# Grouped-query scores of the first block as three split products, their halves made in the second gate stage

## The reference, cut to what matters

```
def attend(q, k, v, scale):
    s = jnp.einsum("bqkgd,blkd->bkgql", q, k).astype(jnp.float32) * scale
    p = jax.nn.softmax(s, axis=-1).astype(v.dtype)
    return jnp.einsum("bkgql,blkd->bqkgd", p, v)
...
    k_gqa = rms_norm(k_g.reshape(b, l, GQA_KV_HEADS, GQA_DIM), lp["g_kn_gqa"])
    q_gqa = rms_norm(q_g.reshape(b, l, GQA_HEADS, GQA_DIM), lp["g_qn_gqa"])
...
    oc_gqa = attend(qc_gqa, k_gqa_c, v_gqa_c, GQA_DIM ** -0.5)
```

## Time and profile before

| | |
|---|---|
| time, median of 3 runs (lowest, highest) | 2534.72 us (2531.97, 2537.26) |
| profiled execution: span from first to last instruction | 2534.4 us |
| profiled execution: own time | not listed apart from its span |
| TensorE busy | 2434.9 us, 96% |
| VectorE busy | 1635.4 us, 65% |
| ScalarE busy | 1318.0 us, 52% |
| GpSimd busy | 405.1 us, 16% |
| mean granted TensorE clock | 0.993 of full |

### The profile page before, as it was taken

One profiled execution on the slowest core, in us unless ns is written; L12 is line 12 of the kernel. 1 busy time (PEld: TensorE's weight loads), 2 busy tenths in 40 slices (PEclk: granted clock), 3 DMA queues, 4 the chain that ended last, 5 costly groups with the idle time before them and its releaser, 6 DMA issues. The chain is left out here.

```text
span 2534.4 us, 45823 instructions
## 1 busy us (share of the span) xinstructions
PE 2434.9 (96%) x17406; PEld 2158.2 (85%) x17406; DVE 1635.4 (65%) x2537; ACT 1318.0 (52%) x2157; POOL 405.1 (16%) x354
## 2 busy tenths in 40 slices
PE   6999999999899999999999999998999999999997
PEld 5876899898599988875899899887998799769986
DVE  3664787567577857774788466546665666576655
ACT  3444566454546645545466455445554554465544
POOL 1210211221031121111301211020110211011102
PEclk9999999999999999999999999999999999999999
DMA  8576466566245655474556566563466466535663
GB/s 277 187 228 213 152 192 193 167 190 205 78 134 175 200 168 162 151 241 164 161 182 192 175 219 201 163 207 109 136 198 199 150 199 203 162 101 161 195 202 116
DMA packets 332956, 450.43 MB, mean 178 GB/s; under 512 B 28192, under 2 KB 207392, under 8 KB 332768
## 3 DMA queue, kind: packets, MB, share of 16 engines
q1 hardware_dynamic: 332400, 446.32, 55.9%
q0 software_dynamic: 368, 1.57, 0.2%
HBM read 446.73 MB, written 1.05 MB: 177 GB/s over the span
## 5 line engine op out<-in xcount | busy, mean ns | idle before, releaser
L771 DVE TENSOR_TENSOR wlo<-raw,whi 128x1024 fp32r<-128x1024 f32 (+2 forms) x706 | 845.2, 1215 | 589.4 <-ACT whi L765 585.4
L765 ACT CAST whi<-raw 128x1024 fp32r<-128x1024 f32 (+2 forms) x776 | 768.1, 1007 | 637.2 <-PE S L1065 233.7
L1086 PE MATMUL S<-hhi,whi 128*128 128x256 f32 x1943 | 538.4, 277 | 1.4 <-ACT b_kT L1394 0.9
L1086 PE MATMUL S<-hlo,whi 128*128 128x256 f32 x1943 | 536.5, 277 | 1.2 <-DVE hlo L2054 1.1
L1086 PE MATMUL S<-hhi,wlo 128*128 128x256 f32 x1943 | 536.5, 277 | 0.0
L1086 PEld LDWEIGHTS S<-hhi,whi 128*128 128x128 f32 x1943 | 365.2, 188 | 2.4 <-ACT b_kT L1394 1.1
L1086 PEld LDWEIGHTS S<-hlo,whi 128*128 128x128 f32 x1943 | 365.1, 188 | 1.8 <-DVE hlo L2054 1.7
L1086 PEld LDWEIGHTS S<-hhi,wlo 128*128 128x128 f32 x1943 | 365.1, 188 | 0.0
L1086 PE MATMUL G<-hhi,whi 128*128 128x256 f32 x1084 | 301.1, 278 | 0.4 <-ACT hhi L1456 0.4
L1086 PE MATMUL G<-hlo,whi 128*128 128x256 f32 x1084 | 298.1, 278 | 0.1
L1086 PE MATMUL G<-hhi,wlo 128*128 128x256 f32 x1084 | 297.9, 277 | 0.0
(11 more groups left out here) (404 smaller groups left out, 4336.0 us busy)
## 6 DMA issues: line engine op xcount, KB each, us to landing
raw<-in_ffn_wi SPq DMA_DIRECT2D x352, 256.0 KB, 3.5
raw<-in_w_up SPq DMA_DIRECT2D x264, 256.0 KB, 3.8
modw<-in_w_mod SPq DMA_DIRECT2D x192, 256.0 KB, 4.6
raw<-in_w_in SPq DMA_DIRECT2D x192, 256.0 KB, 3.0
raw<-in_ffn_wo SPq DMA_DIRECT2D x160, 256.0 KB, 3.5
raw<-in_w_down SPq DMA_DIRECT2D x120, 256.0 KB, 3.5
raw<-in_a_wqkv SPq DMA_DIRECT2D x72, 256.0 KB, 3.1
raw<-in_w_o SPq DMA_DIRECT2D x48, 256.0 KB, 3.2
```

The source lines that it names most:

```text
L765: act.copy(whi[:, n0 % SPLIT, z, w], raw[:, n0 % RAW, z, w]).then_inc(hi_done, 1)
L771: eng.tensor_tensor(wlo[:, n0 % SPLIT, z, w], raw[:, n0 % RAW, z, w], whi[:, n0 % SPLIT, z, w].bitcast(F32), ALU.subtract)\
L1086: mm = pe.matmul(o, w, x, start=first and c == 0 and m == 0 and z == 0, stop=last and c == kc - 1 and z == len(terms) - 1, skip_group_chec ...
```

## The change

The grouped keys and queries get high and low halves of their own. On ScalarE, at the start of the second gate stage and ahead of its first slot, two casts make `kghi` and `qghi`; they wait until the products of `uq` and the transposes of `gqat` are done. On VectorE, in the same stage behind the nine low halves of the weights and ahead of the rest of the row work, two subtractions make the low halves, in place of `kgT` and `qgT` (for the context, whose keys are needed again by the latent stream, the keys' low half goes to the second half of `kghi`). Both high halves lie in memory that is free between `uq` and the Fourier product behind the attention. In the attention the score of a grouped head is the sum of three fp32r products, (high q, high k), (high q, low k), (low q, high k), alternating between the two heads; one wait for `grouped_lo` is added ahead of them, the wait for `exp_done` is the same as before. The latent heads are unchanged.

```diff
@@ tensors
+            ("kghi", 0, [P, 4 * T], F32R), ("qghi", 7 * T, [P, GQA_H // 2, T], F32R),
...
+             ("b1_qglo", o1["qgT"], [P, GQA_H // 2, T], F32R),
+             ("b1_kglo", o1["kgT"], [P, GQA_KV, 2 * T], F32R),
@@ helper
+        def grouped_keys(st):
+
+
+            x = kgT[:, :, 0:st.blocks * P]
+            if st.s == LAT:
+                return x, kghi[:, :].rearrange("p (e n) -> p e n", e=GQA_KV), kglo[:, :, :]
+            both = kghi[:, :].rearrange("p (z e n) -> p z e n", z=2, e=GQA_KV)
+            return x, both[:, 0], both[:, 1]
@@ TensorE, attention
+                def grouped_scores(s):
+
+
+                    c, g = pairs_[s // 2][1], 2 * pairs_[s // 2][1] // (GQA_H // GQA_KV)
+                    rows_q = slice(s % 2 * P, (s % 2 + 1) * P)
+                    _, k_hi, k_lo = grouped_keys(st)
+                    pe.wait_ge(grouped_lo, 2 * owns.index(st) + 2)
+                    pe.wait_ge(exp_done, 2 * (st.a + s - 1))
+                    for z, (q, k) in enumerate(((qghi, k_hi), (qghi, k_lo), (qglo, k_hi))):
+                        for j in range(2):
+                            lo, s0 = slice(j * DH, (j + 1) * DH), (2 * (s % 2) + j) * SN
+                            mm = pe.matmul(S[:, s0:s0 + nb * P], q[lo, c, rows_q], k[lo, g], start=z == 0, stop=z == 2,
+                                           skip_group_check=True)
+                    mm.then_inc(s_done, 1)
...
                     name, c, _ = pairs_[s // 2]
+                    if name == "gqa":
+                        grouped_scores(s)
+                        return
...
-                        elif name == "gqa":
-                            parts.append([(qgT[lo, c, rows_q], kgT[lo, 2 * c // (GQA_H // GQA_KV), 0:nb * P])])
@@ ScalarE, gates
+                    if st.part:
+
+                        uq, gqat = before(st, "uq"), before(st, "gqat")
+                        act.wait_ge(bank_done[1], uq.n + uq.counts["n"])
+                        for q in range(gqat.tk, gqat.tk + gqat.counts["tk"]):
+                            act.wait_ge(tr_free[q % 2], q // 2 + 1)
+                        keys, k_hi, _ = grouped_keys(own_of(st))
+                        act.copy(k_hi, keys).then_inc(grouped_hi, 1)
+                        act.copy(qghi[:, :, :], qgT[:, :, :]).then_inc(grouped_hi, 1)
@@ VectorE, gates
                     over_units(dve, st, lambda k, j, i: split_weights(st, j, i, k, lo_and_rows))
+                    if st.part:
+                        own = own_of(st)
+                        keys, k_hi, k_lo = grouped_keys(own)
+                        for z, (x, hi, to) in enumerate(((keys, k_hi, k_lo), (qgT[:, :, :], qghi[:, :, :], qglo[:, :, :]))):
+                            dve.wait_ge(grouped_hi, 2 * owns.index(own) + z + 1)
+                            dve.tensor_tensor(to, x, hi.bitcast(F32), ALU.subtract).then_inc(grouped_lo, 1)
                     for _ in rows_work:
                         pass
```

More of the change, by code:

```diff
@@ L425, in build @@
             ("modw", 0, [P, 2 * MOD_SLOTS, SK, SN], F32)])
-        xn, gtB, crT, av, rsB, diag2, junk = region(3 * D, [
+        xn, gtB, crT, av, rsB, diag2, kghi, qghi, junk = region(3 * D, [
             ("xn", 0, [P, NT, D], F32), ("gtB", NT * D, [P, D], F32), ("crT", 0, [P, 2, 5, T], F32R),
             ("av", 0, [P, 2, 2, T], F32), ("rsB", 4 * T, [P, T], F32), ("diag2", 5 * T, [P, NT, P], F32),
+            ("kghi", 0, [P, 4 * T], F32R), ("qghi", 7 * T, [P, GQA_H // 2, T], F32R),
             ("junk", 6 * T, [P, 2, T], F32)])
@@ L448, in build @@
         o2, n2 = offsets(sizes)
-        (qkv1, qT1, qgT, gT, kT1, kgT, v1, vg, oThi1, oTlo1, fThi1, fTlo1,
+        (qkv1, qT1, qgT, gT, kT1, kgT, v1, vg, qglo, kglo, oThi1, oTlo1, fThi1, fTlo1,
          qkvA, qkvB, kdupB, sgate, sgained, qT2, kT2, sm, mask, order, pT, phi, plo, oThi2, oTlo2, fThi2, fTlo2) = region(max(n1, n2), [
@@ L547, in build @@
         exp_done = sem("exp_done")
+        grouped_hi = sem("grouped_hi")
+        grouped_lo = sem("grouped_lo")
         rden_ready = sem("rden_ready")
@@ L639, in follows_mod, with own_of @@
             return st.kind == "gates" and st.part == 1
+        def own_of(st):
+            return next(z for z in STAGES[STAGES.index(st):] if z.kind == "attn")
+        owns = [st for st in STAGES if st.kind == "attn" and st.name == "own"]
+        def grouped_keys(st):
[4 more added lines that the diff above has]
+            return x, both[:, 0], both[:, 1]
         def value_bank(st, p):
```

## The result

The changed kernel takes 2547.88 us (median of 5 runs, 2546.47 to 2548.76); the kernel before, measured beside it, 2534.72 us (2531.97 to 2542.36). The ratio is 1.0051, with a 95% interval of 1.004 to 1.0061: 13 us slower, between 10 and 15.5. The recorded execution spans 2546.1 us against 2534.4, 11.7 more. The device time of an execution is a little longer than its span: 2547.88 against 2546.1 here, and by 1.8 to 2.1 us in the executions of the kernel before whose span is known. So the recorded execution of the kernel before took about 2536.3 us (an estimate from that difference), 1.6 us more than the median; its span can't be set against the median as was done ahead. This would explain why the spans differ by less than the medians.

The account below looks back on a forecast made before the run. TensorE, busy for 96% of the span, was taken as the bound. Waits of +10.1, scores of -2.0 and clock of +3.0 us sum to +11.1 on the recorded 2534.4: 2545.5 us, range 2538.5 to 2551.5.

Parts of the forecast that it names:

- Casts on the chain: Second gate stage: ScalarE's two new casts start VectorE's chain 1.9 us later in each latent stream, 1.5 in the context.
- Subtractions on the chain: VectorE, ahead of the last row work: two subtractions add 2.4 us in each latent stream, hidden in the context.
- The latent seam: Between second gate stage and attention: `rows_ready` comes 4.3 us later, all paid by TensorE, twice, 8.6 us.
- Scores: Grouped attention steps on TensorE: three split products save 0.15 us (latent) or 0.06 (context) a step, 2.0 us in all.
- Clock: TensorE's clock falls to half in or behind the wait at both latent seams, 1.5 us each, +3.0 us.
- the first: Rival: no new fall of the clock at the latent seams; +8.1 us, 2542.5 us, chance 0.15.
- the fifth: Rival: casts and subtractions fall into gaps at the seam and only the saving is left; 2532.4 us, chance 0.03.
- The second: Rival: grouped scores on TensorE pay back 8.2 us, clock kept; +1.9 us, 2536.3 us, not slower, chance 0.14.
- The third: Rival: grouped products run one behind another, steps grow by 0.32 and 0.08 us; +16.8 us, 2551.2 us, chance 0.08.
- the fourth: Rival: weight loads of grouped products are not hidden, 0.42 and 0.51 us lost; +21.2 us, 2555.6 us, chance 0.04.

Follow-up runs that it names:

- the two kernels with halves in gaps: The change with casts late on ScalarE, subtractions on VectorE behind its parts of attention steps 0 and 2: 2534.87 us with split products, 2534.48 with two fp32 products.
- the run with GpSimd: The change with casts late on ScalarE and subtractions moved from VectorE to GpSimd: 2544.14 us, ratio 1.0036 to the kernel before.

## Why the prediction was right

The time predicted was 2545.5 us, slower; measured were 2547.88, inside the range. The 2545.5 were counted from the recorded span, so the number to set beside it is the span of the changed kernel, 2546.1. Step by step, by the two recorded executions:

- **Casts on the chain.** 1.9 us predicted for the first low half in the latent stream, 1.90 measured (3.16 - 1.26). In the context 1.5 predicted; its Fourier product is later by 1.63 - 0.13 = 1.50.
- **Subtractions on the chain.** 2.4 predicted, 2.29 measured. In the context they are hidden, as predicted: VectorE still waits 3.21 us for the Fourier product behind them.
- **The latent seam.** 4.3 predicted in each layer; measured 5.47 - 1.28 = 4.19 and 10.80 - 6.63 = 4.17. The sum was right, the wait was not: I forecast the whole of it as TensorE's wait, "about 5 us, not 0.8". It is 3.75, since 1.25 falls on the products of the stage's last slots, which are set by the same chain. The run that moved the casts alone shows the same split. The two edits together, moved off the chain, remove the whole loss, which settles that it is this chain.
- **Scores.** A step of 0.91 (512 columns) and 0.58 (256) was predicted; the free steps of layer 1 take 0.89, those of the context 0.55 (201.95 to 202.50) in place of 0.64. The failing part is the share that reaches the end. I took 2.0 us, "nearer the upper end"; by the timelines of the two kernels with halves in gaps it is 1.2. In layer 0 nothing is left, as TensorE then waits for ScalarE's copies in six of the eight steps, and in layer 1 only every second step counts.
- **Clock.** One stretch at half behind each latent seam, as predicted, 1.02 + 1.16 = 2.2 us in place of 3.0. Filling the wait takes both away. That it would fall at both was argued from longer idle time alone, and the 3.10 us without a fall show that this reason isn't enough.

The parts as measured, 1.5 + 4.2 + 4.2 + 2.2 - 1.2, make 10.9, where 11.1 was predicted. That they are so near is in part luck: the clock was taken 0.8 us too dear and the products' saving 0.8 us too high, and the two misses cancel. The spans differ by 11.7. By the table the other 0.8 us lie ahead of the first layer (0.13), in the stretch from the context's Fourier product to 533 us (0.35 come back there, not the 0.56 of the products), from the attention of layer 0 to layer 1 (0.14), and behind layer 1's attention (0.33); no run gives them a cause.

Of the rivals, the first (no fall of the clock) is refuted by the stretches at 0.53 and 0.52, the fifth by the waits. The second, that the scores pay it back, needs 5.0 us; the two runs with halves in gaps differ by 0.4 us the other way, and their timelines show 1.2 us saved. The third and the fourth, products one behind another or with open loads, fall by the rows: the step has become shorter. The weight loads of the new products take 0.183 us (ns: least, median, most):

```profile
L1195 PEld LDWEIGHTS S<-kghi,qghi x64: 182/183/286, 201.9 to 1200.0; 64*128 64x128 f32 x64
```

and yet the third product of a head follows the second by 0.23 us (1183.53 to 1183.76; the second follows the first by 0.34). The section "The mechanism" of "TensorE: Matmul & The Clock Gate" in the Trainium skill lists that a load overlaps running products only where the row groups differ; taken alone, this would have each load wait, and the trace doesn't agree, the load is hidden. The section itself also names a background weight buffer into which a load may go ahead of running products, which would allow what the trace shows. The same section of the Trainium skill shows products in different rows running at the same time; there the trace agrees, the products of the two heads start together (x2 in one row at 1183.19).

## What to carry over

Work on a half-idle engine costs its full length if it stands ahead of a chain without slack, and the idle time it makes can halve TensorE's clock besides (it did behind the 3.75 us here); so put it where that engine waits for the bound one, as long before its use as that allows (here that alone turned 13 us of loss into none). A saving on the bound engine counts only in the steps in which it is the bound: count the waits step by step before it is multiplied.

## What was not expected of the hardware

GpSimd's subtractions of two operands held up VectorE's instructions with two operands until they ended. In the context's stage of the run with GpSimd too, two instructions beside GpSimd's subtractions (1.30 and 3.09 us) take 2.08 and 3.01 us, in place of 0.95 and 0.96:

```profile
156.88 2.08 DVE L1934 TENSOR_TENSOR pp<-pp,rs 128x768 f32<-128x768 f32 x1
158.99 3.01 DVE L1935 TENSOR_TENSOR pp<-pp,rows 128x768 f32<-128x768 f32 x1
```

The GpSimd instruction takes longer as well (3.38 and 3.09 us, where the middle one of GpSimd's 55 weight subtractions of that shape takes 2.40 in the kernel before). This could have been read ahead of the run, for the kernel before makes some weights' low halves on GpSimd, and now and then one meets one of VectorE's, which in this instance takes 3.08 us, not 1.22 (GpSimd, then VectorE):

```profile
719.89 3.26 POOL L771 TENSOR_TENSOR wlo<-raw,whi 128x1024 fp32r<-128x1024 f32 x1 [15.07 <-ACT whi L765]
721.15 3.08 DVE L771 TENSOR_TENSOR wlo<-raw,whi 128x1024 fp32r<-128x1024 f32 x1 [0.26 <-ACT whi L765]
```

But GpSimd's power of 128x16 leaves VectorE's work beside it as it was: in the run with GpSimd, one from 601.99 us takes 3.55 us, and VectorE's instructions with two operands beside it take 0.96 and 1.23 us as elsewhere. In the Trainium skill, "SBUF — State Buffer", section "SBUF: two separate sides", says that these two engines share a pair of ports, which one of them holds for a whole instruction while the other waits, and that a VectorE instruction with two inputs from SBUF is concerned. The four stretched instructions of that run agree with it (the first ends 1.1 us, about its own length, behind GpSimd's); no run here tells why the power doesn't do it.

The second surprise is that products in the two halves of the array's rows don't keep the program's order: written head by head, they still start in pairs (x2 in each row from 1160.26 us), and the step takes 0.90 us either way.
